# Chunked delta rule on one core: the next chunk's inversion in the same bursts as the current chunk's solution, side work of VectorE cut into single pieces, group norm by three column groups

## The chip, the cores and the metric

The kernel runs as one program on one core of a Trainium2 chip. The metric is the device time of a run in microseconds (us); lower is better. Engines are called PE (TensorE), DVE (VectorE), ACT (ScalarE), POOL (GpSimd) and SP (SyncE, which here issues nearly all transfers).

## The reference, cut to what matters

One decoder layer over 536 tokens: 16 meta tokens and 512 prompt tokens (528, one sequence with a running state) and 8 sample tokens with a state each.

```
proj = rmsnorm(x) @ w_in                 # RWKV columns | retention columns | gates gA, gB
# branch A, RWKV-7, 8 heads of 64, over the tokens t in order:
sa = S @ (-kk_t);  S = S * w_t + sa (x) (kk_t * a_t) + v_t (x) k_t;  y_t = S @ r_t
yn = (y - mean(y)) * rsqrt(var(y) + LNX_EPS)      # per head, the group norm
ya = (yn * lnx_w + lnx_b + bonus) * g
# branch B: retention, multiplied by swish of its gate
merged = sigmoid(gA) * (ya @ w_branch_a) + sigmoid(gB) * (o @ w_branch_b)
x = x + merged @ w_out
x = x + hierarchical_moe(rmsnorm(x))              # top-1 group, top-2 of 16 experts
```

Everything is float32 but for some tables of the routing.

## The kernel before, in words

Activations lie with channels on partitions and tokens in columns; a width of 536 tokens is worked in two halves of 268 columns (`HT`). One SBUF tensor, `arena`, holds nearly everything, so the trace names it everywhere and the rows are told apart by line and shape.

**One list sets the order.** `order()` writes a list of steps; every engine walks the same list and does its part of each step (PE from L796, ACT from L1140, DVE from L1333). Engines keep together by semaphores only. So a step's place in the list is its place in the in-order queue of PE, of ACT and of DVE. DVE waits for the end of nearly each of its own instructions.

**Jobs and banks.** Steps named `j_...` are jobs: matrix products into PSUM bank 0 or 1 in turn, read by ACT or DVE. PE may open job n when job n-2 has been read (`open_job`).

**Fill.** 32 projection half-tiles (`j_proj` for the gates, 8 contraction steps each) and 16 of `j_bb` (branch B, 4 steps each) need nothing from branch A. They are cut into parts (`pre` and the job itself, L792) of two contraction steps, a float32 matmul of 268 columns each, which the trace records as two; so a part is four records. There are 160 parts. `take(n)` puts the next n of them into the list. They cover the waits of branch A.

**Branch A** runs over 9 chunks (`CHUNKS`: eight of 64 tokens, one of 16). For each chunk c:

- `wk_prep` (issued one chunk ahead): ACT makes two exponentials of the decays, DVE makes four scaled products from them; `wk_k` holds two more (`decayed`).
- `wk_a` (PE L925 to L943, DVE L1485): products of the scaled keys, and two transposes; DVE masks them into `tp` and `ab`.
- `wk_x` and `wk_t` (L961; L971 and L974) for b = 2, 4, 8, 16: the inverse of a unit triangular 32x32 matrix by doubling. PE's 32x32 products of `wk_x` go through DVE (mask, `xl`) to `wk_t`, whose result DVE adds into `tp`, for the next `wk_x`. `wk_k` puts four transposes behind the first `wk_t`.
- `wk_r`, `wk_sa`, `wk_y`, `wk_sb` (L986 to L1016): right-hand side and solution, block by block, each going through ACT (`rr`, `sa`) or DVE (`y1`) before the next.
- `wk_s` (L1026 to L1044): new state `st` (DVE) and output y (ACT).

A new chunk's `wk_a` waited for everything of the chunk before it, since `tp`, `ab`, `kq` and `tok` exist once. In the list one part of fill stands between each two of these steps (three behind `wk_a`). What the small products of one such place take on PE is called a burst here; an unshared 64-token chunk has 13 of them.

**Side work.** The eight sample tokens' state update (`sm_in`, `j_sk`, `j_sv`, `sm_y`, `j_sy` for four pairs of heads, on DVE 128x512 each) is put into the chunks by `take` at ends of jobs, `sm_in` as three DVE instructions in one step. From chunk 6 on it is followed by the group norm of the first 268 columns: `j_mean` and `j_var` (L1062, sums over a head by a matmul), where DVE subtracts and squares, ACT takes the root, DVE takes the reciprocal and does three more passes (L1576 to L1583), all in one step for each of four pairs of heads and each half.

**Behind the chunks**: the rest of the side work, the group norm of the second half, then `j_ba` (branch A's projection, L1075, 8 tiles for each half of the columns, each read and merged by two DVE instructions), then `j_out`, routing and the experts. `w_ba` is loaded when the last chunk is done; the x of the residual and `w_out` behind it.

## Time and profile before

| | |
|---|---|
| median of 3 runs | 997.94 us (996.11, 997.94, 1003.03) |
| time of the profiled execution | 1003.03 us |
| its span, first to last instruction | 1001.1 us |
| its mean granted PE clock | 0.940 |
| busy: PE, DVE, ACT, POOL | 901.9 us (90%), 390.6 (39%), 211.9 (21%), 37.6 (4%) |
| PE L792, projections and fill, 268 columns, float32 | 1600 records, 417.4 us busy, 410 ns each |
| DVE TENSOR_TENSOR out of PSUM, nine forms | 235, 101.8 us busy, 434 ns each, 291.7 us idle before them |
| DMA | 118.81 MB, mean 119 GB/s |

The span in 40 slices of 25 us: busy tenths of PE and DVE, and the granted clock of PE in tenths of full speed.

```profile
PE   5999999898999999899889999978899954999995
DVE  3422055256448843432443443233651134211125
PEclk9999998699899999999999999957899985999998
```

"Busy" of an engine counts its instructions, not its waits. A granted clock of 0.5 over a stretch means that PE ran at 1.2 GHz there, 1.0 that it ran at 2.4 GHz; values between are mixtures. Branch A's chunks begin at 362.8 us (slice 15) and `j_ba`'s second half starts at about 732.2 us.

### The profile page before, as it was taken

Reading aid. Unit: us, or ns where it says so; the run is one execution under the profiler, and the core shown is the slowest. Engines: PE = TensorE matmul, PEld = TensorE weight load, DVE = VectorE, ACT = ScalarE, POOL = GpSimd, SP = SyncE. Lnnn points to the kernel's source line nnn. Section 1 sums busy time; section 2 is a strip of 40 time slices with the busy share of each in tenths; the row PEclk is TensorE's granted clock in tenths of the full one; section 3 lists DMA queues with packets and bytes.
Section 4 is the critical chain, followed back from the end, with each engine's and each line's share of the span. In section 5 each row is a group of like instructions: output and inputs, shape, how many; then the busy total and the mean of one; then the engine's idle time right before and its main releaser. Section 6 shows DMA issues by size and latency. Waiting matters only on the chain. (4 is left out here: it accounts for less than half of the span.)

```text
span 1001.1 us, 20286 instructions
## 1 busy us (share of the span) xinstructions
PE 901.9 (90%) x8942; PEld 620.3 (62%) x8942; DVE 390.6 (39%) x742; ACT 211.9 (21%) x423; POOL 37.6 (4%) x34
## 2 busy tenths in 40 slices
PE   5999999898999999899889999978899954999995
PEld 4777756676667867676667767746688841333331
DVE  3422055256448843432443443233651134211125
ACT  2000210114332122221222132222200240111124
POOL 0000000000000000000000000000000001122223
PEclk9999998699899999999999999957899985999998
DMA  9111101201111111001110100106406228999976
GB/s 357 68 64 61 66 21 43 116 1 64 66 60 59 55 36 34 27 30 34 34 33 34 45 24 24 44 22 218 176 3 270 84 84 316 417 386 392 396 260 223
DMA packets 26998, 118.81 MB, mean 119 GB/s; under 512 B 5328, under 2 KB 7632, under 8 KB 22048
## 3 DMA queue, kind: packets, MB, share of 16 engines
q1 hardware_dynamic: 22592, 106.57, 27.9%
q0 software_dynamic: 4320, 10.95, 3.8%
q8 instruction: 71, 1.16, 0.5%
q14 instruction: 15, 0.12, 0.0%
HBM read 104.24 MB, written 18.05 MB: 122 GB/s over the span
## 5 line engine op out<-in xcount | busy, mean ns | idle before, releaser
L792 PE MATMUL psum<-arena 128*128 128x268 f32 x1600 | 417.4, 410 | 9.4 <-ACT arena L1136 5.8
L792 PEld LDWEIGHTS psum<-arena 128*128 128x128 f32 x1600 | 301.6, 196 | 84.8 <-ACT arena L1136 12.6
L1315 DVE TENSOR_TENSOR arena<-psum,arena 128x268 f32<-128x268 f32 (+8 forms) x235 | 101.8, 434 | 291.7 <-PE psum L1075 58.2
L1136 ACT ACTIVATE arena<-psum 128x268 f32<-128x268 f32 (+6 forms) x174 | 72.1, 419 | 527.9 <-PE psum L792 274.3
L1315 DVE TENSOR_TENSOR arena<-arena 128x268 f32<-128x268 f32 (+10 forms) x212 | 105.7, 498 | 68.8 <-ACT arena L1136 56.2
L1075 PE MATMUL psum<-arena 128*128 128x268 f32 x384 | 92.4, 397 | 2.9 <-DVE arena L1315 2.7
L1828 PE MATMUL psum<-arena 128*32 128x512 f32 (+1 forms) x640 | 87.4, 609 | 5.1 <-DVE arena L1981 5.1
L1075 PEld LDWEIGHTS psum<-arena 128*128 128x128 f32 x384 | 72.9, 193 | 19.4 <-DVE arena L1315 4.5
L1981 DVE TENSOR_TENSOR arena<-psum,arena 128x256 f32<-128x256 f32 (+1 forms) x36 | 24.0, 691 | 110.6 <-ACT arena L1895 106.1
L1828 PEld LDWEIGHTS psum<-arena 128*32 128x32 f32 (+1 forms) x640 | 25.6, 117 | 63.4 <-issue 59.4
L1136 ACT ACT_TABLE_LOAD x36 | 46.2, 1283 | 31.4 <-PE psum L792 21.0
L1318 DVE SCALAR_TENSOR_TENSOR arena<-arena 128x268 f32<-128x268 f32 (+4 forms) x93 | 46.4, 499 | 2.7
L1742 POOL DMA_INDIRECT arena<-u_rows,ids x12 | 12.4, 1036 | 895.4 <-DVE ids L2017 833.5
L1860 PE MATMUL psum<-arena 128*32 128x512 f32 (+1 forms) x288 | 40.2, 595 | 0.0
L1318 DVE SCALAR_TENSOR_TENSOR arena<-psum,arena 128x268 f32<-128x268 f32 x24 | 10.5, 439 | 63.5 <-PE psum L819 47.2
L1234 ACT ACTIVATE arena<-psum 64x256 f32<-64x256 f32 (+1 forms) x54 | 20.4, 378 | 64.3 <-PE psum L950 32.7
L961 PEld LDWEIGHTS psum<-arena 32*32 32x32 f32 (+1 forms) x1072 | 11.8, 105 | 22.4 <-issue 13.5
L971 PE MATMUL psum<-arena 32*32 32x32 f32 (+1 forms) x800 | 12.0, 195 | 15.1 <-DVE arena L1315 15.0
L971 PEld LDWEIGHTS psum<-arena 32*32 32x32 f32 (+1 forms) x800 | 9.1, 109 | 26.5 <-DVE arena L1315 20.4
L1860 PEld LDWEIGHTS psum<-arena 128*32 128x32 f32 (+1 forms) x288 | 10.8, 115 | 21.3 <-issue 21.3
L1580 DVE RECIPROCAL arena<-arena 128x268 f32<-128x268 f32 x8 | 14.6, 1829 | 23.6 <-ACT arena L1136 23.4
L1136 ACT ACTIVATE arena<-psum,arena 128x268 f32<-128x268 f32 (+2 forms) x37 | 19.0, 535 | 20.8 <-PE psum L804 10.5
(181 smaller groups left out, 727.0 us busy)
## 6 DMA issues: line engine op xcount, KB each, us to landing
arena<-in_w_gu SPq DMA_DIRECT2D x16, 2048.0 KB, 21.6
arena<-in_w_in SPq DMA_DIRECT2D x46, 512.0 KB, 3.5
arena<-in_w_dn SPq DMA_DIRECT2D x16, 1024.0 KB, 19.3
...
```

The costliest lines, as they stand in the source:

```text
L792: last = mm(ps, wt[:, i % NW, k, :], rhs[:, k, cols(hf)], start=(k == 0), stop=(k == nk - 1))
L971: mm(psum[g, 2560 + H * p:2560 + H * p + n], tp[g, 1, p, 0:n], xl[g, p, 0:n], start=True, stop=True)
L1075: last = mm(ps, w[:, m, k, :], x[:, k, cols(hf)], start=(k == 0), stop=(k == nk - 1))
L1136: run(nc.scalar.activation(out, in_, fn, **kw), s)
L1234: nc.scalar.activation(tok[part, i, :, :], src, ACT.Copy).then_inc(s_toks if s else s_act, 1)
L1315: run(v.tensor_tensor(out, a, b, op), s)
L1318: run(v.scalar_tensor_tensor(out, a, sc_, b, op0, op1), s)
L1580: run(v.reciprocal(x, x))
L1742: pool.indirect_dma_start(ug[:, e % 2, :], None, u2_dram, bass.IndirectOffsetOnAxis(ap=ids[:, e:e + 1], axis=0), bounds_check=T - 1, oob_i ...
L1828: last = mm(bank(2 + i % 2)[part], ue[:, i % 2, k, part], w_gu[x % NWE][:, k, :], start=(k == 0), stop=(k == KD - 1))
L1860: last = mm(bank(down_bank(e) + q)[part], hht(e)[:, f, part], w_dn[x % NWE][:, f, 512 * q:512 * q + 512], start=(f == 0), stop=(f == 1))
L1981: v.tensor_tensor(out, x, y, op).then_inc(s, 1)
```

## The change

It does six things.

1. **Two chunks at once.** `tp`, `ab`, `kq`, `tok` get a second buffer, and the output of `wk_y` moves to another PSUM bank. The solution and the state of chunk c (`wk_r`, `wk_sa`, `wk_y`, `wk_sb`, `wk_s`) are no longer behind its own inversion but inside that of chunk c+1: `wk_x` 2 with `wk_r`, `wk_t` 2 and `wk_k` with `wk_sa`, `wk_x` 4 with `wk_y`, `wk_t` 4 with `wk_sb`, `wk_x` 8 with `wk_s`. A 64-token chunk has 9 bursts then. The last chunk's solution stands alone behind it.
2. **Fill.** 16 parts for each chunk where there were 15: two at five of the nine places, three behind `wk_a`, one behind `wk_x` 4, `wk_t` 8 and `wk_x` 16; 6 instead of 8 before the first `wk_a`.
3. **`wk_prep` and `wk_k` on DVE in single instructions**: `wk_p` 0 to 3 and `wk_d` 0 and 1, one or two per place; the two exponentials (`wk_e`) stand behind `wk_sa`. The decayed old state (`wk_sp`) has a step of its own.
4. **Side work in single instructions**: `sm_in` becomes `sm_a` 0 to 2, the second instruction of each sample job becomes `sm_b`, `sm_c`, `sm_d`. At most one goes to a place (up to three behind the last `wk_t`).
5. **Group norm by three column groups** (`UNITS`): columns 0 to 268 for each pair of heads, 268 to 512 for two pairs at once, and the last 24 columns of all four: 7 `j_mean` and 7 `j_var` instead of 8 and 8. The square moves from DVE to ACT. The reciprocal is cut into pieces (`ln_r`, 134 or 122 columns), and the passes behind it (`ln_w`, `ln_b`, `ln_g`) are single steps. `j_ba` of the second half waits for all seven units.
6. **`w_ba` in two transfers**: the first half, 1 MB, when `j_bb` is done, the second where the whole was.

```
-        w_ba = at(KD * NP * P, KD, NP, P, start=raw0)
+        tp = [at(2 * NP * H, 2, NP, H), tp2]
+        ab = [at(NP * 2 * C, NP, 2, C), ab2]
+        kq = [at(NP * 2 * C, NP, 2, C), kq2]
+        tok = [at(3 * NP * C, 3, NP, C), tok2]
+        w_ba = [at(2048, KD // 2, NP, P, start=x) for x in (base - 4 * T - RH * T, raw0)]
...
+UNITS = [(p, p + 1, 0, HT) for p in range(NP)] + [(0, 2, HT, SEQ), (2, 4, HT, SEQ), (0, NP, SEQ, T)]
+PIECES = [2] * NP + [4, 4, 1]
...
-        s += [("wk_a", c)] + take(3)
-        if c + 1 < len(CHUNKS):
-            s += [("wk_prep", c + 1)]
-        for b in LEVELS[1:]:
-            if b < w:
-                s += [("wk_x", c, b)]
-                if 2 * b >= min(w, H):
-                    s += [("wk_r", c)]
-                s += take(1) + [("wk_t", c, b)]
-                if b == 2:
-                    s += [("wk_k", c)]
-                s += take(1)
-        s += [("wk_sa", c)] + take(1)
-        if w > H:
-            s += [("wk_y", c)] + take(1) + [("wk_sb", c)] + take(1)
-        s += [("wk_s", c)] + take(1)
+        s += [("wk_a", c + 1)] + take(3, 1)
+        s += [("wk_x", c + 1, 2)] + r + take(2, 1)
+        s += [("wk_t", c + 1, 2), ("wk_k", c + 1)] + sa + ([("wk_sp", c)] if c >= 0 else [])
+        s += ([("wk_e", c + 2)] if c + 2 < len(CHUNKS) else []) + take(2, 1)
+        s += [("wk_x", c + 1, 4)] + y + take(1)
+        s += [("wk_t", c + 1, 4)] + sb + prep(c + 2, ("wk_p", 0)) + take(2, 1)
+        s += [("wk_x", c + 1, 8)] + st + prep(c + 2, ("wk_p", 1)) + take(2, 1)
+        if c == 5:
+            while not whole_job():
+                s += take(1)
+            s += [("j_var", n) for n in range(NP)]
+            side += [x for n in range(NP) for x in norms(n)]
+        s += [("wk_t", c + 1, 8)] + prep(c + 2, ("wk_d", 0)) + take(1)
+        if 16 in lev:
+            s += [("wk_x", c + 1, 16)] + prep(c + 2, ("wk_p", 2)) + take(1)
+            s += [("wk_t", c + 1, 16)] + prep(c + 2, ("wk_p", 3), ("wk_d", 1)) + take(2, 1) + beside(3)
...
+    side += [("j_mean", 4), ("j_mean", 5)]
+    s += r + take(2, 2) + sa + [("wk_sp", len(CHUNKS) - 1)] + take(2, 2) + st
+    side += [("j_mean", 6), ("j_var", 4), ("j_var", 5)] + norms(4) + [("j_var", 6)] + norms(5) + norms(6)
...
                 elif kind == "wk_r":
                     pe.wait_ge(s_st, c + 1)
-                    pe.wait_ge(s_toks, 3 * c + 3)
+                    pe.wait_ge(s_toks, 3 * c + (5 if c + 1 < NCH else 3))
...
                 elif kind == "wk_y":
                     pe.wait_ge(s_sa, 2 * c + 1)
+                    pe.wait_ge(s_tri, 3 * c + 6)
...
                 elif kind == "wk_s":
                     pe.wait_ge(s_sa, 2 * c + (2 if CHUNKS[c][1] > H else 1))
+                    if c + 1 < NCH:
+                        pe.wait_ge(s_toks, 3 * c + 6)
...
                     if kind == "j_ba":
-                        pe.wait_ge(s_ba, 16)
-                        pe.wait_ge(s_ya, NP * (hf + 1))
+                        pe.wait_ge(s_ba[m // 4], 16)
+                        pe.wait_ge(s_ya, len(UNITS) if hf else NP)
```

The order of PE's matmuls from the last transposes of a chunk on, before. L792 is fill; a row's x2 is a part (a matmul here is two records of the trace). L961 is `wk_x`, L971 and L974 `wk_t`, L950 `wk_k`, L1051 a sample job. First the beginning of chunk 2's inversion:

```order
L943 MATMUL psum<-arena 64x128 x8
L792 MATMUL psum<-arena 128x268 x6
L961 MATMUL psum<-arena 32x32 x16
L792 MATMUL psum<-arena 128x268 x2
L971 MATMUL psum<-arena 32x32 x16
L974 MATMUL psum<-arena 32x32 x16
L950 MATMUL psum<-arena 64x128 x4
L792 MATMUL psum<-arena 128x268 x2
L961 MATMUL psum<-arena 32x32 x16
```

and the end of the same chunk, where L1000 is `wk_sa`, L1008 `wk_y`, L1016 `wk_sb`, each with fill on both sides:

```order
L974 MATMUL psum<-arena 32x32 x16
L792 MATMUL psum<-arena 128x268 x2
L1000 MATMUL psum<-arena 32x64 x8
L792 MATMUL psum<-arena 128x268 x2
L1008 MATMUL psum<-arena 32x64 x8
L792 MATMUL psum<-arena 128x268 x2
L1016 MATMUL psum<-arena 32x64 x8
L792 MATMUL psum<-arena 128x268 x2
```

The same engine after the change, in chunk 2's inversion from `wk_t` 2 on, with chunk 1's solution in it (L852 is fill, L1023 `wk_x`, L1033 and L1036 `wk_t`, L1012 `wk_k`, L1064 `wk_sa`, L1073 `wk_y`, L1081 `wk_sb`):

```order
L852 MATMUL psum<-arena 128x268 x4
L1033 MATMUL psum<-arena 32x32 x16
L1036 MATMUL psum<-arena 32x32 x16
L1012 MATMUL psum<-arena 64x128 x4
L1064 MATMUL psum<-arena 32x64 x8
L852 MATMUL psum<-arena 128x268 x4
L1023 MATMUL psum<-arena 32x32 x16
L1073 MATMUL psum<-arena 32x64 x8
L852 MATMUL psum<-arena 128x268 x2
L1033 MATMUL psum<-arena 32x32 x16
L1036 MATMUL psum<-arena 32x32 x16
L1081 MATMUL psum<-arena 32x64 x8
```

`wk_sa`, `wk_y` and `wk_sb` have moved into bursts of the next chunk, and there are two parts of fill where there was one, but for the place between `wk_x` 4 and `wk_t` 4.

DVE at such places. Before, between the masks of `wk_a` in chunk 4 and the mask of its first `wk_x` (the 128x128 row), with the semaphores waited for; first the two instructions of a sample job, then four rows of `wk_prep` for chunk 5, waiting for ACT by `s_e`:

```order
L1315 TENSOR_TENSOR arena<-psum,arena 128x512 [waits s_job]
L1568 TENSOR_REDUCE arena<-arena 128x8 [waits s_free0]
L1315 TENSOR_TENSOR arena<-arena 128x256 [waits s_ps,s_e,s_ys]
L1315 TENSOR_TENSOR arena<-arena 128x256 [waits s_dve]
L1318 SCALAR_TENSOR_TENSOR arena<-arena 128x4x64 [waits s_dve]
L1315 TENSOR_TENSOR arena<-arena 128x4x64 [waits s_dve]
L1315 TENSOR_TENSOR arena<-psum,arena 128x128 [waits s_pt,s_ab]
```

After, from the mask of `wk_x` 4 in chunk 3 to that of `wk_x` 8 (the two 128x128 rows):

```order
L1385 TENSOR_TENSOR arena<-psum,arena 128x128 [waits s_pt]
L1385 TENSOR_TENSOR arena<-psum,arena 128x256 [waits s_py,s_rr,s_xl]
L1385 TENSOR_TENSOR arena<-psum,arena 128x256 [waits s_pr]
L1385 TENSOR_TENSOR arena<-arena 128x256 [waits s_e,s_tt]
L1385 TENSOR_TENSOR arena<-arena 128x512 [waits s_free1,s_dve]
L1385 TENSOR_TENSOR arena<-psum,arena 128x128 [waits s_pt,s_ws]
```

The one instruction that waits for the exponentials now stands behind the add of `wk_t` 4, with one piece of side work after it; `wk_prep` is no longer ahead of a mask as a block.

PE behind the chunks, before (L1062 is `j_mean` and `j_var`, L1075 `j_ba` and `j_out`):

```order
L792 MATMUL psum<-arena 128x268 x8
L1075 MATMUL psum<-arena 128x268 x4
L1062 MATMUL psum<-arena 128x268
L1075 MATMUL psum<-arena 128x268 x4
L1062 MATMUL psum<-arena 128x268
```

and after (L1126 `j_mean`, L1131 `j_var`, L1143 `j_ba` and `j_out`), from the last chunk's `wk_s` on:

```order
L852 MATMUL psum<-arena 128x268 x6
L1126 MATMUL psum<-arena 128x96
L1131 MATMUL psum<-arena 128x488 x2
L852 MATMUL psum<-arena 128x268 x8
L1143 MATMUL psum<-arena 128x268 x4
L1131 MATMUL psum<-arena 128x96
L1143 MATMUL psum<-arena 128x268 x76
```

Only 14 matmuls of fill (seven parts) are left behind `wk_s` of the last chunk, where 44 were.

## Rows read from the trace of the kernel before

**Rows 1.** Table by stretch: start:end, length, busy us (count) per engine, PE clock, DMA share.

```profile
362.80:650.00 287.20, 267.23 (x5644) 200.17 (x5644) 111.69 (x249) 71.84 (x147) 0.00 (x0) 0.98 0.10 33
650.00:655.20 5.20, 1.45 (x10) 0.90 (x8) 3.56 (x5) 1.97 (x4) 0.00 (x0) 1.00 0.00 0
655.20:683.00 27.80, 25.08 (x238) 17.24 (x239) 5.09 (x10) 5.73 (x8) 0.00 (x0) 0.51 0.10 31
683.00:711.80 28.80, 24.56 (x97) 18.47 (x96) 11.90 (x18) 8.46 (x12) 0.00 (x0) 0.94 0.49 179
711.80:732.20 20.40, 17.55 (x63) 13.14 (x62) 16.50 (x27) 3.14 (x5) 0.00 (x0) 0.83 0.60 216
850.00:1001.10 151.10, 135.66 (x1030) 47.09 (x1022) 37.76 (x57) 34.58 (x65) 34.21 (x27) 0.97 0.90 346
```

**Rows 2.** Waits of PE, 362.8 to 732.2 us: total us, times, longest.

```profile
PE psum L971 <- DVE arena L1315: 15.0, 10, 3.1
PE psum L961 <- DVE arena L1315: 6.6, 3, 3.8
...
PE psum L792 <- ACT arena L1136: 1.8, 4, 1.0
```

**Rows 3.** PE in order of time, chunk 2: start, duration, instruction, idle before.

```profile
443.52 0.45 PE L961 MATMUL psum<-arena 32*32 32x32 f32 x32
443.90 1.17 PE L792 MATMUL psum<-arena 128*128 128x268 f32 x4
447.50 0.65 PE L971 MATMUL psum<-arena 32*32 32x32 f32 x32 [2.43 <-DVE arena L1315]
```

**Rows 4.** DVE over the same stretch.

```profile
445.31 0.89 DVE L1315 TENSOR_TENSOR arena<-arena 128x256 f32<-128x256 f32 x2 [2.98 <-ACT arena L1136]
...
447.16 1.02 DVE L1315 TENSOR_TENSOR arena<-psum,arena 128x128 f32<-128x128 f32 x2
```

**Rows 5.** ACT over the same stretch.

```profile
443.20 1.28 ACT L1136 ACT_TABLE_LOAD   x1
444.49 0.73 ACT L1136 ACTIVATE arena<-arena 128x256 f32<-128x256 f32 x2
```

**Rows 6.** DVE groups, 362.8 to 732.2 us: busy us, mean ns, idle before.

```profile
L1315 DVE TENSOR_TENSOR arena<-arena 128x512 f32<-128x512 f32 x24 | 16.6, 692 | 2.1 <-ACT arena L1136 1.4
...
L1315 DVE TENSOR_TENSOR arena<-psum,arena 128x128 f32<-128x128 f32 x45 | 13.2, 293 | 31.0 <-PE psum L974 15.5 <-PE psum L961 14.7
```

**Rows 7.** PE in order of time, bursts and fill without waits.

```profile
426.04 1.17 PE L792 MATMUL psum<-arena 128*128 128x268 f32 x4
427.14 0.45 PE L974 MATMUL psum<-arena 32*32 32x32 f32 x32
...
440.71 2.88 PE L792 MATMUL psum<-arena 128*128 128x268 f32 x12
...
453.26 0.45 PE L971 MATMUL psum<-arena 32*32 32x32 f32 x32
453.54 0.48 PE L974 MATMUL psum<-arena 32*32 32x32 f32 x32
...
460.10 0.45 PE L961 MATMUL psum<-arena 32*32 32x32 f32 x32 [1.36 <-DVE arena L1315]
460.49 0.33 PE L986 MATMUL psum<-arena 64*64 64x64 f32 x4
```

**Rows 8.** DVE groups of the group norm, 650 to 732 us, columns as above.

```profile
L1580 DVE RECIPROCAL arena<-arena 128x268 f32<-128x268 f32 x8 | 14.6, 1829 | 23.6 <-ACT arena L1136 23.4
L1318 DVE SCALAR_TENSOR_TENSOR arena<-arena 128x268 f32<-128x268 f32 x16 | 8.0, 499 | 0.6
```

**Rows 9.** ACT in order of time: two roots of the group norm.

```profile
684.98 0.86 ACT L1136 ACTIVATE arena<-psum,arena 128x268 f32<-128x268 f32 x2
```

**Rows 10.** PE in order of time, behind the chunks: one `j_ba`.

```profile
711.79 1.97 PE L1075 MATMUL psum<-arena 128*128 128x268 f32 x8
713.60 0.61 PE L1062 MATMUL psum<-arena 128*128 128x268 f32 x2
```

337 lines of the change are left out of this document (202 added, 135 removed).

## Prediction

> **What bounds the kernel now.** The page first: PE is busy for 901.9 of 1001.1 us, DVE for 39%, ACT for 21%. So the time is PE's own work, plus its waits, plus what it loses where its clock is granted at half. The change touches one stretch, from the first chunk at 362.8 us to the second half of `j_ba` at 732.2 us, and the table by stretch [rows 1] cuts it in five. Length less busy time gives PE's idle time: 20.0, 3.7, 2.7, 4.2 and 2.9 us, 33.5 together. The clock column gives the rest. A clock of 0.98 over 287.2 us loses 2% of it, 5.7 us. Between 655.2 and 683 us it is 0.51, nearly all at 1.2 GHz, though PE is busy for 25.1 of 27.8 us: 0.49 x 27.8 = 13.6, less half of the 2.7 us in which PE did nothing anyway, 12.3 us. The fall stands behind the longest wait (3.8 us, [rows 2]). The last two stretches lose 0.06 x 28.8 = 1.7 and 0.17 x 20.4 = 3.5, less half of some idle time, 2.8. Low clock: 22.5 us. Waits and clock make 56.0 us, the most that better cover can give back.
>
> Whom PE waits for says the list of waits [rows 2]: DVE, at `wk_t` (L971, ten times, 15.0 us) and `wk_x` (L961, 6.6 us). One such wait in order of time shows why. PE ends a part of fill and is ready for `wk_t` at 445.07, but starts at 447.50 [rows 3]. DVE's mask for it is the first of two instructions at 447.16 [rows 4]. Ahead of that mask stands `wk_prep`, four instructions that begin at 445.31 after 2.98 us of waiting for ACT. ACT was loading its table and making the two exponentials, 443.20 to 445.22 [rows 5]. So a 0.29 us mask is late because a block of four instructions and a chain through ACT stand in front of it in an in-order queue; elsewhere it is the block of `sm_in`. DVE is not short of time, its work is in the wrong order.
>
> **The change, part by part.**
>
> *The waits in the chunks (20.0 us idle, 5.7 us clock).* The exponentials now follow `wk_sa` and their first reader stands behind the add of `wk_t` 4. Between the two PE does two parts of fill, `wk_x` 4 with `wk_y`, one part, and `wk_t` 4: 2.0 + 0.7 + 1.1 + 0.6 = 4.4 us with fill at 1.0 to 1.1 and a small product at 0.3 to 0.4 [rows 7], against ACT's 1.2 us for three copies (0.37 each if they cost as an exponential) and 2.0 us for load and exponentials [rows 5]. Covered. DVE's longest queue between a product and the next that needs it: behind `wk_x` 2 mask 0.29, mask of `kq` 0.69 and one piece 0.69, 1.7 us [rows 6], while PE does `wk_r` and two parts (2.0). Behind `wk_x` 4, `wk_t` 8 and `wk_x` 16 only one part, 1.10 us from start to start (426.04 to 427.14, [rows 7]), covers a mask of 0.29 or an add of 0.44 [rows 4] and the product of `wk_prep` behind it, 0.9 us at most. That holds, but with 0.2 us to spare. The three pieces behind the last `wk_t` (2.1 us) have two parts and 3.5 us of `wk_a` above them. The shared bursts add waits for ACT: `wk_r` for the four copies of the new chunk, made during three parts of fill, and `wk_y` for the copy behind `wk_sa`, two parts earlier. Both are done. I leave 4 us of the 25.7: the 1.8 us for ACT at banks [rows 2], which sample jobs between two fills still cause, and 2.2 us for places with 0.2 us to spare. Bounds: 1.8, and half of the 20.0, 10.
>
> *Fewer bursts.* A part alone takes 1.10 us, but three in a row 2.81 (440.71 to 443.52), 0.94 each: going over from small tiles to 128x128 costs 0.16. Thirty-two records of 32x32 products take 0.38 before fill (443.52 to 443.90), but 0.28 with more such products behind them (453.26 to 453.54): 0.10 for going the other way [rows 3, 7]. So 0.26 us for a burst with its stretch of fill, 0.13 for a border. With 13 bursts becoming 9 that would be 4 x 0.26 x 8 chunks = 8.3 us. But a burst that mixes tile sizes keeps borders inside: `wk_x` is followed by `wk_r` after 0.39 us (460.10 to 460.49), as long as by fill [rows 7]. Counting changes of tile size, a chunk had 22 and has 16: 6 x 0.13 x 8 = 6.2 us. I take 6.2. The Trainium skill (TensorEngine Tiling, Key Properties) says that "changing tiling mode (not just tile) drains the TensorE", which speaks against a part of this change, since three of the five shared bursts change mode inside. By the rule the gain is 6.2 us, without it 8.3; the 0.39 us row agrees with the rule.
>
> *The stretch of low clock (3.7 and 2.7 us idle, 12.3 us clock).* The wait of 3.8 us at 651.5 us came from `j_var` of the first half: reciprocal 1.83, two passes 1.03, product 0.44, one block of 3.3 us [rows 4, 8], in front of a mask. After, that is five instructions of 0.9 us or less, one for a place at most times. The wait goes, and I take it that the clock then stays up: all 18.7 us. In its place come four `j_var` in a row in chunk 6. Banks 0 and 1 alternate, so the third waits until ACT has read the first, behind the reading of the projection (0.4), a table load (1.28) and a root (0.43 to 0.5, [rows 5, 9]): 2.2 us after the projection's end, with 1.1 us of PE work before (two jobs): 1.2 us lost.
>
> *Behind the chunks (7.1 us idle, 4.5 us clock).* Laid out from T, the end of the last but one half-tile of fill. PE does `j_mean` 6 (0.2), waits 0.3 for ACT to have read the fill, does `j_var` 4 and 5 (0.95 each, two banks of nearly 500 columns) and is ready at T + 2.4. The bank comes free with ACT's root: reading 0.4, square 0.2, table load 1.28, root of 488 columns about 0.65 [rows 5, 9], with gaps T + 2.8. So 0.7 us lost. Four parts more (3.7) end at T + 6.5, and the eight `j_ba` of the first half, 1.81 us each (711.79 to 713.60, [rows 10]), with `j_var` 6 at T + 21.2. DVE begins at T + 2.8: reciprocals of 976 columns at 1829/268 = 6.8 ns, 6.7 us [rows 8]; of 96 columns, 0.7; eight passes over 244 columns at 0.44, 3.5; two products of 488, 1.3; nine short instructions for the 24 columns, 1.4; sixteen of 0.44 for `j_ba`, 7.0; and 45 gaps of 0.03, 1.4. That is 22.0 us, to T + 24.8. PE waits 0.7 us at the second `j_ba`, since the block of unit 4 stands ahead of the first one's reader, and then 24.8 - 21.9 = 2.9 us for the last unit, before `j_ba` of the second half. Waits: 0.7 + 0.7 + 2.9 = 4.3 us. PE was slow behind a wait of 2.4 us (L971 took 0.65 where 0.45 is usual, [rows 3, 7]), so 2.0 us of clock more. Bounds of the two together: 2 and 10. `j_mean` and `j_var` take 0.6 us less in all, two starts of a job.
>
> By the Trainium skill (ScalarE: Activation LUTs, What ACT_TABLE_LOAD costs) a load comes with a drain, 2.66 us in all. The row shows 1.29 us from load to the next instruction [rows 5]; by the page's figure the two roots above would come 1.4 us later each, an estimate of 2.8 us more. I go by the row.
>
> *Transfers and the beginning.* The 1 MB of `w_ba` goes ahead of a projection tile that is wanted two tiles of fill later. Its second half has some 15 us. With six parts instead of eight `wk_a` starts as DVE's products end; nothing lost or won. Experts are loaded after `j_ba` and `j_out`, so their transfers move up with the rest.
>
> **Sum.** Given back 33.5 + 22.5 + 6.2 + 0.6 = 62.8 us. New or left: 4 + 1.2 + 4.3 + 2.0 = 11.5 us. Net 51.3 us. The profiled execution took 1003.03 us, the slowest of the three (median 997.94); since most of what differs between runs should lie in waits and clock that now go, I count from 1003.03 itself: 951.7 us, or 952.
>
> **The rivals.**
>
> *Forecast, chance 0.70.* With its own bounds: chunk waits 1.8 to 10, tail 2 to 10, clock of the first stretch +-1.4, borders 6.2 to 8.3: 942 to 964.
>
> *The waits move (0.19).* Single cover of 1.10 us fails where a piece of side work or of the norm stands in front of the mask, or the tail is DVE-bound: seven parts of fill are left behind the chunks where 22 were, and DVE's 22 us stand against 18.8 us of PE work. For it: the 0.2 us margin. Against it: DVE has 12 us of work in a chunk of 31. If half of the chunk waits stay (10 and 3 of clock instead of 4) and the tail waits as long as before (7.1 + 4.5 instead of 6.3), that is 9 + 5.3, about 966; with the low clock of 27.8 us coming back at one wait over 3 us, up to 978.
>
> *The clock stays low whatever the order (0.05).* PE was busy nine tenths of the 27.8 us and did not get its clock back [rows 1]. If low stretches belong to the small products and not to the wait, the 22.5 us stay: 952 + 22 = 974.
>
> *No gain (0.03).* The last stage moves its data at 0.90 DMA share [rows 1]. If those transfers did not move up with the rest, the gain would vanish there: about 1000. Against: nothing in it is issued by time, all behind semaphores of `j_ba` or `j_out`.
>
> *Slower (0.03).* Five shared bursts per chunk tie the chain through ACT to the inversion. If each waited for ACT, the 51 us would be gone at 51/40 = 1.3 us each, the length of one table load [rows 5] ahead of a copy; at 1.8 us each, 952 + 72 = 1024 us.
>
> **How the numbers follow.** The likeliest case gives 952. Reaching up into the second case until about 2 in 10 are left out, and down to the forecast's own lower bound, the range is 941 to 968. About 1% is what a measurement of this kernel can tell from no change: faster by over 1% means under 988, which the first three cases give: 0.94; within 1% 0.03; slower 0.03.
>
> **What would show it.** The chunks' PE waits for DVE fall from 20 to under 6 us in 280; no stretch of 20 us stands at 0.5; a chunk has nine bursts and takes about 31 us; the longest PE wait is at the first `j_ba` of the second half, for `ln_g`, about 3 us. Wrong would be: waits of over 1 us at `wk_x` or `wk_t` in most chunks, PE waiting for ACT at `wk_r` or `wk_y`, or low clock without a wait in front.

## The result, and the profile after

| kernel | median us | lowest to highest | profiled run | its span | its mean clock |
|---|---|---|---|---|---|
| before | 1000.49 | 996.11 to 1006.0 | 1003.03 | 1001.1 | 0.940 |
| after | 961.94 | 957.59 to 969.43 | 963.45 | 961.9 | 0.954 |

The ratio is 0.962, with a 95% interval from 0.954 to 0.970. The change takes 38.6 us off the median and 39.6 us off the profiled run. The forecast was 952 us, 51.3 us less than the profiled run of before. So the sign and the range (941 to 968) held, and 11.7 us of the forecast gain, over a fifth, stayed out. Where they went can be read from the trace.

The table by stretch of after, from the first chunk to the end of `j_ba`, columns as in [rows 1]:

```profile
361.60:500.00 138.40, 138.10 (x2894) 106.20 (x2895) 70.04 (x145) 40.53 (x79) 0.00 (x0) 1.00 0.12 37
500.00:512.00 12.00, 9.50 (x146) 6.37 (x145) 2.61 (x6) 4.37 (x7) 0.00 (x0) 0.72 0.01 1
512.00:560.00 48.00, 47.91 (x1071) 37.87 (x1070) 18.53 (x43) 11.00 (x24) 0.00 (x0) 1.00 0.19 63
560.00:595.00 35.00, 30.98 (x596) 23.02 (x594) 9.28 (x23) 12.76 (x23) 0.00 (x0) 0.95 0.11 33
595.00:650.00 55.00, 55.00 (x1140) 43.18 (x1140) 25.13 (x55) 14.14 (x33) 0.00 (x0) 1.00 0.10 31
650.00:667.00 17.00, 16.51 (x129) 11.21 (x127) 2.02 (x4) 4.58 (x9) 0.00 (x0) 0.80 0.40 120
667.00:692.20 25.20, 18.80 (x82) 15.37 (x83) 22.48 (x44) 4.17 (x6) 0.00 (x0) 0.99 0.71 268
692.20:772.80 80.60, 80.60 (x371) 65.53 (x372) 15.76 (x44) 6.89 (x10) 0.00 (x0) 0.96 0.27 111
```

The first 138 us of the chunks run without a gap and at full clock: PE is busy for 138.10 of 138.40 us, where the whole chunk stretch of before had 20.0 us of idle time at a clock of 0.98 [rows 1]. The stretch of 27.8 us at 0.51 is gone. What is left sits in three places, which the list of waits of after names (361.6 to 692.3 us; total, times, longest, as in [rows 2]):

```profile
PE psum L1143 <- DVE arena L1385: 6.1, 2, 4.9
PE psum L852 <- ACT arena L1204: 3.3, 3, 2.5
PE psum L1126 <- ACT arena L1204: 2.9, 1, 2.9
PE psum L1131 <- ACT arena L1204: 1.4, 2, 1.1
```

L1143 is `j_ba`, L852 fill, L1126 and L1131 `j_mean` and `j_var`. No `wk_x` or `wk_t` is in the list. PE waits for ACT in the chunks instead. PE in order of time around 504 us, and ACT over the same stretch:

```profile
499.56 1.17 PE L852 MATMUL psum<-arena 128*128 128x268 f32 x4
500.57 1.02 PE L1118 MATMUL psum<-arena 128*128 128x512 f32 x2
504.09 2.15 PE L852 MATMUL psum<-arena 128*128 128x268 f32 x4 [2.50 <-ACT arena L1204]
```

```profile
499.90 0.39 ACT L1204 ACTIVATE arena<-psum 128x256 f32<-128x256 f32 x1
500.31 1.28 ACT L1204 ACT_TABLE_LOAD   x1
501.60 0.73 ACT L1204 ACTIVATE arena<-arena 128x256 f32<-128x256 f32 x2
502.35 1.28 ACT L1204 ACT_TABLE_LOAD   x1
503.64 0.40 ACT L1204 ACTIVATE arena<-psum 128x268 f32<-128x268 f32 x1
```

The fill at 499.56 ends a half-tile of projection, and ACT is to read it with a sigmoid so that the bank comes free. A sample job follows at once, then the next half-tile, which wants that bank. ACT has just begun `wk_e`: table load, two exponentials, table load back. The reader starts at 503.64, and PE goes on at 504.09 after 2.50 us of waiting, with the clock down (the next part of fill, four records, takes 2.15 us instead of 1.17). The same picture stands in chunk 6 at 571.10 us, where `j_mean` waits 2.91 us.

The third place is the end of the first half of `j_ba`, PE in order of time:

```profile
664.91 1.91 PE L1131 MATMUL psum<-arena 128*128 128x488 f32 x4 [0.29 <-ACT arena L1204]
667.35 3.88 PE L852 MATMUL psum<-arena 128*128 128x268 f32 x16 [0.53 <-ACT arena L1204]
...
674.37 12.91 PE L1143 MATMUL psum<-arena 128*128 128x268 f32 x56 [1.14 <-DVE arena L1385]
692.20 13.00 PE L1143 MATMUL psum<-arena 128*128 128x268 f32 x43 [4.92 <-DVE arena L1385]
```

DVE is busy for 22.48 of the 25.2 us before it (the last row but one of the table by stretch).

**A ruler for the experiments.** The medians of one kernel differ by up to 6 us from chip to chip (955.9 and 961.9 for the changed kernel), and the first chunk of these kernels starts anywhere between 363.6 and 372.0 us, though nothing ahead of it differs: between 10 and 300 us the clock varies by itself (0.88 over 100 to 200 us in e0_after; 0.96, 0.87 and 0.96 over 10 to 100, 100 to 200 and 200 to 300 us in e9_norm_late, where e0_after has 1.00 in the first and the last). So beside each median stands the **rest**: the span less the start of the first `wk_a`. Kernels without a long wait repeat it within 0.6 us (e1: 581.2 and 581.3; e5, e6 and e10: 575.7 to 576.3). The changed kernel, whose waits bring low clock in one run and not in another, does not (594.7 and 589.6).

| kernel | median us | ratio, 95% interval | first `wk_a` | rest |
|---|---|---|---|---|
| before | 1000.49 | | 370.31 | 630.8 (two parts of fill, some 2 us, more lie ahead of it) |
| after | 961.94 | 0.962 [0.954, 0.970] | 367.19 | 594.7 |
| e0_after | 955.88 | 0.957 [0.951, 0.962] | 363.62 | 589.6 |
| e1_exp_late | 949.18 | 0.949 [0.944, 0.954] | 365.50 | 581.2 |
| e1_again | 952.08 | 0.950 [0.946, 0.954] | 369.17 | 581.3 |
| e2_apart | 959.49 | 0.961 [0.955, 0.967] | 363.79 | 592.9 |
| e3_norm_early | 960.04 | 0.958 [0.953, 0.963] | 369.25 | 590.9 |
| e5_tail | 944.51 | 0.941 [0.937, 0.945] | 364.47 | 575.7 |
| e6_split | 946.26 | 0.943 [0.937, 0.948] | 368.42 | 576.3 |
| e7_own | 953.26 | 0.950 [0.947, 0.954] | 367.82 | 583.7 |
| e8_blocks | 951.09 | 0.950 [0.948, 0.951] | 369.56 | 581.7 |
| e9_norm_late | 965.32 | 0.962 [0.959, 0.965] | 372.02 | 595.3 |
| e10_spread | 946.19 | 0.944 [0.943, 0.946] | 371.75 | 575.9 |
| e11_own_blocks | 975.82 | 0.977 [0.973, 0.982] | 367.13 | 608.0 |

### The profile page after: what moved, and what is told of

It is laid out like the page before. It is cut to its first block and busy times, and to the rows that moved or that the text cites. A ratio compares the mean times of both kernels' runs of the same rounds, so it can differ in the third digit from the quotient of the medians.

```text
span 961.9 us, 20304 instructions
## 1 busy us (share of the span) xinstructions
PE 882.5 (92%) x8938; PEld 612.1 (64%) x8938; DVE 390.4 (41%) x748; ACT 212.3 (22%) x427; POOL 37.3 (4%) x34
## 5 line engine op out<-in xcount | busy, mean ns | idle before, releaser
L852 PE MATMUL psum<-arena 128*128 128x268 f32 x1600 | 404.2, 404 | 10.8 <-ACT arena L1204 7.3
L852 PEld LDWEIGHTS psum<-arena 128*128 128x128 f32 x1600 | 299.5, 194 | 91.7 <-ACT arena L1204 14.8
L1385 DVE TENSOR_TENSOR arena<-arena 128x268 f32<-128x268 f32 (+11 forms) x203 | 102.1, 503 | 62.4 <-ACT arena L1204 51.6
L1143 PE MATMUL psum<-arena 128*128 128x268 f32 x384 | 92.7, 399 | 6.1 <-DVE arena L1385 6.1
L1143 PEld LDWEIGHTS psum<-arena 128*128 128x128 f32 x384 | 73.6, 195 | 22.0 <-issue 6.6
L1388 DVE SCALAR_TENSOR_TENSOR arena<-arena 128x268 f32<-128x268 f32 (+6 forms) x101 | 48.2, 477 | 3.0
L1204 ACT ACT_TABLE_LOAD x34 | 43.6, 1283 | 10.1 <-DVE arena L1529 7.7
L1388 DVE SCALAR_TENSOR_TENSOR arena<-psum,arena 128x268 f32<-128x268 f32 (+2 forms) x23 | 10.4, 451 | 68.2 <-PE psum L879 47.2
L1204 ACT ACTIVATE arena<-arena 128x256 f32<-128x256 f32 (+11 forms) x56 | 21.8, 412 | 8.3 <-DMA arena<-in_x 3.3
L1984 ACT ACTIVATE arena<-psum 128x256 f32<-128x256 f32 x12 | 4.6, 387 | 84.8 <-PE psum L1917 84.8
L1204 ACT ACTIVATE arena<-psum,arena 128x268 f32<-128x268 f32 (+4 forms) x36 | 18.6, 542 | 13.4 <-PE psum L864 9.9
L1023 PEld LDWEIGHTS psum<-arena 32*32 32x32 f32 (+1 forms) x1072 | 12.1, 108 | 13.0 <-issue 13.0
L1893 PE MATMUL psum<-arena 128*128 128x128 f32 x96 | 13.5, 286 | 6.1 <-DMA arena<-u_rows,ids 6.1
```

Of the source, the lines that this page charges most:

```text
L852: last = mm(ps, wt[:, i % NW, k, :], rhs[:, k, cols(hf)], start=(k == 0), stop=(k == nk - 1))
L1023: last = mm(psum[g, 2304 + H * p:2304 + H * p + n], ab[c % 2][g, p, 0, rd], tp[c % 2][g, 0, p, 0:n], start=True, stop=True)
L1143: last = mm(ps, w[:, k, :], x[:, k, cols(hf)], start=(k == 0), stop=(k == nk - 1))
L1204: run(nc.scalar.activation(out, in_, fn, **kw), s)
L1385: run(v.tensor_tensor(out, a, b, op), s)
L1388: run(v.scalar_tensor_tensor(out, a, sc_, b, op0, op1), s)
```

## The experiments

### Where the missing gain went

**e0_after** is the changed kernel itself.

> The changed kernel itself, for comparison on this chip. Its trace on record shows 13.8 us of PE idle time between 361.6 and 692.2 us and 11.8 us of low clock up to 772.8 us. Both theories expect the same picture: waits for ACT of 2.5 us in chunk 4 and 2.9 us in chunk 6 behind a table load and two exponentials, and 4.9 us for DVE ahead of the second half of the branch projection. A ratio to the kernel before of about 0.96.

It repeats every wait of after within 0.1 us. Its rest is 5.1 us shorter than that of after, because the clock stayed up behind the wait in chunk 4 (34.6 us from `wk_a` to `wk_a` instead of 37.4) and over parts of the tail.

**e1_exp_late** moves the exponentials behind the parts that follow `wk_sa`:

```
-        s += ([("wk_e", c + 2)] if c + 2 < len(CHUNKS) else []) + take(2, 1)
+        s += take(2, 1) + ([("wk_e", c + 2)] if c + 2 < len(CHUNKS) else [])
```

> One change to the changed kernel: the two exponentials of the next chunk stand behind the two parts of fill that follow wk_sa, not ahead of them. My theory: the two new waits of PE (2.5 us in chunk 4, 2.9 us in chunk 6) come from ACT, which must load a table, make the exponentials and load the table back before it reads the projection whose bank PE needs next. Both waits go, and with them the low clock behind them (3.4 and 1.7 us): 10 us less than the changed kernel, within 8 to 11. Rival: the banks are the cause (a job right behind a projection), the reading is late anyway, and the exponentials, now later, hold up DVE's first product: the waits stay at 2 us or more and new ones of about 1 us appear at wk_x 8 in each chunk, 0 to +8 us.

Measured: 949.18 us, 6.7 under e0_after and so less than the 8 to 11 us expected; the rest is 8.3 us shorter. The longest waits of PE in e1_again, the same kernel, 355 to 770 us:

```profile
PE psum L1143 <- DVE arena L1385: 6.1, 2, 4.9
PE psum L961 <- DVE arena L1385: 2.1, 1, 2.1
PE psum L1131 <- ACT arena L1204: 1.4, 2, 1.1
```

The waits of 2.5 and 2.9 us are gone and nothing came in their place (the 2.1 us at L961 stand before the first chunk, in after too). Of the 8.3 us, 6.9 lie in the chunks (247.2 us from the first `wk_a` to the last, against 254.1 in e0_after): 5.4 us of waiting, and the rest low clock behind it. The other 1.4 us lie behind the chunks, where the two kernels are the same. So one position of one step on ACT cost 6.9 us in e0_after, and 9.8 in after (257.0 us), where the clock also fell behind the wait in chunk 4.

**e3_norm_early** begins the norm of units 4 and 5 earlier: their means right behind the state of chunk 7, their variances ahead of the last `wk_s`.

```
+        if c == 7:
+            while not whole_job():
+                s += take(1)
+            s += [("j_mean", 4), ("j_mean", 5)]
...
-    side += [("j_mean", 6), ("j_var", 4), ("j_var", 5)] + norms(4) + [("j_var", 6)] + norms(5) + norms(6)
+    s += [("j_var", 4), ("j_var", 5)] + take(1, 1) + st
+    side += norms(4) + [("j_mean", 6), ("j_var", 6)] + norms(5) + norms(6)
```

> The changed kernel with the means of the 244-column groups right behind the state of chunk 7 (a projection half-tile earlier) and their variances ahead of the last chunk's state. My theory: the 4.9 us wait before the second half of the branch projection and the 1.1 us at its second job come from DVE being the bound there, 22 us of its work starting at the first root; started 5 to 6 us earlier, the two waits fall from 6.0 to about 1 to 2 us and the low clock behind them (3.2 us) goes: 6 us less than the changed kernel, within 3 to 8. Rival: DVE's work is bound by PE's jobs that it must read one after the other, the wait only moves ahead: under 2 us of difference.

A miss: the time is 4.2 us and the rest 1.3 us longer than that of e0_after, and PE still waits 4.73 us ahead of the second half (4.91 in e0_after). The rest alone would be a weak witness here, since the clock behind the last `wk_s` stood at 0.66 over 10 us in this run and at 0.83 in e0_after, which is 1.7 us; the wait that stayed is the finding. DVE in order of time shows why it stayed:

```profile
664.25 0.67 DVE L1391 TENSOR_TENSOR arena<-arena 128x488 f32<-128x488 f32 x1
670.00 0.26 DVE L1394 SCALAR_TENSOR_TENSOR arena<-psum,arena 128x96 f32<-128x96 f32 x1 [5.08 <-PE psum L1132]
672.28 0.44 DVE L1391 TENSOR_TENSOR arena<-psum,arena 128x268 f32<-128x268 f32 x1 [2.03 <-PE psum L1149]
```

DVE finished unit 4 at 664.9 us and then stood still for 5.08 and 2.03 us. Unit 5 was ready, but in program order it stood behind the mean of unit 6 and the first `j_ba`, for which DVE had to wait. Starting work early gains nothing while the queue order puts a later arrival ahead of what comes after it.

**e5_tail** (with e1_exp_late's edit) has the same early jobs and puts the norms of both units beside the last parts of fill, ahead of the mean of unit 6:

```
+    late = norms(4) + norms(5)
+    while fill:
+        s += late[:3] + take(1)
+        del late[:3]
+    s += late
+    side[:] = [("j_var", 6)] + norms(6)
+    s += [("j_mean", 6)]
```

The counter that paces side work beside the last fill and `j_ba` (`credit`) starts at -1.5 here instead of 0.

> The kernel of e1_exp_late once more, as partner for the next two on the same chip: 949 us, ratio 0.949, the wait of 6 us for the units' evictions in the column-group norm's tail still there.

> e1_exp_late, and in the tail the mean jobs of units 4 and 5 go right after the state of chunk 7, their variance jobs ahead of the last wk_s, and the norms of both units all lie beside the last parts of the projections, ahead of the mean of unit 6; only unit 6 is normed beside the first half of j_ba. Theory (VectorE's 24.7 us of work without a gap from the root of unit 4 to the first j_ba of the second half is what PE waits for there, and e3_norm_early left it because unit 5 still stood beside j_ba, with VectorE idle for 7 us before): VectorE ends its work ahead of the second half some 7 us earlier against PE, the wait of 4.9 us and the clock lost behind it (3.4 us in 670 to 690) go, 941 to 943 us. Rival (the wait only moves again, as in e3): PE waits about as long at j_ba's second or third job, whose bank VectorE has not emptied because units 4 and 5 stand ahead of it: 946 to 950 us.

Measured 944.51 us, between the theory's 941 to 943 and the rival's 946 to 950. Its partner e1_again came out at 952.08 on the same chip, 3 us above the 949 that was expected of it; the difference is 7.6 us, as the theory had it, and the rest is 5.6 us shorter. The longest waits of PE in e5_tail, 355 to 770 us, without the one of 9.2 us that belongs to the stage behind:

```profile
PE psum L864 <- ACT arena L1216: 1.1, 2, 0.8
PE psum L1143 <- ACT arena L1216: 1.1, 1, 1.1
PE psum L1155 <- DVE arena L1400: 1.0, 1, 1.0
```

and PE in order of time:

```profile
660.01 2.07 PE L1155 MATMUL psum<-arena 128*128 128x268 f32 x8 [0.98 <-DVE arena L1400]
662.67 32.79 PE L1155 MATMUL psum<-arena 128*128 128x268 f32 x144 [0.39 <-DVE arena L1397]
```

The rest of `j_ba` and the beginning of `j_out`, 144 records, now run in one piece. The theory holds; the rival's wait at the first jobs exists but is 1.0 us. With e1_exp_late's edit and this one the kernel is at 0.941 [0.937, 0.945] of before: the fastest of all, 59 us under the median of before on the same chip (1003.47).

**e10_spread**: e5_tail with the four `j_var` of chunk 6 in two pairs.

> e5_tail with the four variance jobs of chunk 6 in two pairs, one whole projection apart, so that the third need not wait for the root of the first. Theory: the wait of 1.1 us for ScalarE in chunk 6 goes and nothing else moves, about 1 us less than e5_tail, which the time can hardly show; it serves as e5_tail's repetition beside the two above: 942 to 946 us. Rival: the later roots delay the norms into the tail, 1 to 3 us more.

The wait of 1.1 us is gone and the chunk is 36.5 instead of 37.1 us long, but 0.4 us more of waiting stands elsewhere, and the rest is the same (575.9 and 575.7). It can stand as a repetition of e5_tail.

### Which part of the change brings the gain in the chunks

Two things were changed there together: DVE's work in single pieces, and two chunks that share bursts. The next three undo one or both.

**e2_apart** keeps two chunks in flight but gives each solution step a place of its own between two parts of fill, with the same 16 parts. Five steps leave the 9 shared bursts, so it has 14 (the expectation says 13):

```
-        s += [("wk_x", c + 1, 2)] + r + take(2, 1)
+        s += [("wk_x", c + 1, 2)] + take(1, 1) + r + take(1)
```

and so on for the other four.

> The changed kernel with the solution's five steps taken out of the shared bursts: wk_r, wk_sa, wk_y, wk_sb and wk_s each stand alone between two parts of fill inside the next chunk's inversion, 13 bursts for a chunk again with the same 16 parts. Everything else is as in the changed kernel. My theory (a price of 0.13 us for each change of tile size, 6 more in a chunk): a chunk without waits, 30.9 us from wk_a of chunk 2 to that of chunk 3, takes 31.7 us; in all 6 us more than the changed kernel. Rival 1 (the price is for a burst, 0.26 us each): 31.9 us, 8 us in all. Rival 2 (the shared bursts matter because the two parts of fill behind each cover DVE): with single parts DVE waits return, 1 us or more per chunk, 15 us or more in all. Rival 3: sharing brings nothing, 30.9 us.

Chunk 2 is 32.8 us long against 30.9 in e0_after, but it has six products of 128x512 for the sample jobs where that has four. Where both have six (chunk 3: 32.8 and 31.8), and in chunk 5 and 7 (30.2 and 29.2), the difference is 1.0 us for five bursts, 0.20 us each. Rival 1's 31.9 us came true, but for another count: at its price of 0.26 us five bursts would cost 1.3. The theory's 0.13 us for a change of tile size comes closer; five separate bursts have seven changes more, 0.9 us. DVE waits did not return (rival 2). The whole kernel is only 3.6 us slower than e0_after, since the edit also takes away the two waits for ACT; against e1_exp_late, which has none of them either, the stretch from the first `wk_a` to the last is 7.1 us longer (254.3 and 247.2).

Where the 0.20 us come from can be read at one burst, `wk_x` 2 and `wk_r` of chunk 2. Shared, in e5_tail (L1035 `wk_x`, L1062 `wk_r`, L864 fill, L1045 the next `wk_t`), PE in order of time:

```profile
428.82 0.45 PE L1035 MATMUL psum<-arena 32*32 32x32 f32 x32
429.20 0.33 PE L1062 MATMUL psum<-arena 64*64 64x64 f32 x4
...
430.28 2.08 PE L864 MATMUL psum<-arena 128*128 128x268 f32 x8
432.28 0.45 PE L1045 MATMUL psum<-arena 32*32 32x32 f32 x32
```

and apart, in e2_apart (L1023 `wk_x`, L1050 `wk_r`, L852 fill, L1033 `wk_t`):

```profile
428.29 0.45 PE L1023 MATMUL psum<-arena 32*32 32x32 f32 x32
428.67 1.17 PE L852 MATMUL psum<-arena 128*128 128x268 f32 x4
429.77 0.33 PE L1050 MATMUL psum<-arena 64*64 64x64 f32 x4
...
430.85 1.17 PE L852 MATMUL psum<-arena 128*128 128x268 f32 x4
431.95 0.45 PE L1033 MATMUL psum<-arena 32*32 32x32 f32 x32
```

Shared, the whole takes 3.46 us, apart 3.66. All of the 0.20 us is on the side of the fill: two parts in a row take 2.00 us from start to start, two single ones 1.10 each. On the other side nothing is saved, for `wk_x` is followed after 0.38 us, by `wk_r` as by fill. It is otherwise where both steps use 32x32 tiles: the second product of `wk_t` 4 is followed after 0.29 us by `wk_sb` (438.32 to 438.61 in e5_tail) and after 0.41 by fill (438.38 to 438.79 in e2_apart).

**e7_own** solves each chunk in its own turn, as before, with all single pieces kept (and the exponentials late):

```
+    for c in range(len(CHUNKS)):
...
+            s += [("wk_x", c, 16)] + r + prep(c + 1, ("wk_p", 2)) + take(1)
+            s += [("wk_t", c, 16)] + prep(c + 1, ("wk_p", 3), ("wk_d", 1)) + take(1, 1)
+        s += sa + [("wk_sp", c)] + take(1)
+        if w > H:
+            s += y + take(1) + sb + take(1, 1)
```

> The changed kernel with the exponentials late, but each chunk solved in its own turn as in the kernel before, in bursts of its own (14 instead of 9 in a chunk of 64), one part of other work between each; VectorE's side work and the preparation stay in single pieces, the group norm stays by column groups. What is left out of the change is thus only that inversion and solution share bursts. Theory (most of the chunks' gain is VectorE's work in single pieces; sharing only saves borders and leaves more cover): no waits for VectorE over 0.5 us in the chunks, a chunk of 32.5 to 33 us as in e2_apart, against 30.9; 957 to 963 us, thus 8 to 14 above e1. Rival (without sharing the chain through a chunk is too tight for the cover of one part a step): PE waits for VectorE again, 10 us or more over the chunks, 970 to 980 us.

(It has 13 bursts, not 14.) Measured 953.26 us, under the expected 957 to 963, and not the rival's 970 to 980. It is 1.2 us above e1_again, where 8 to 14 were expected. But the edit did more than take the sharing away: 12 parts of fill lie behind the last `wk_s` (48 records) where after has 7 (28), and PE waits for DVE at `j_ba` only 0.7 us in all, where e1_again waits 6.1. Between 366 and 650 us PE waits for DVE nowhere:

```profile
PE psum L856 <- ACT arena L1205: 1.6, 3, 0.6
PE psum L1132 <- ACT arena L1205: 1.1, 1, 1.1
PE psum L1127 <- ACT arena L1205: 0.9, 1, 0.9
```

So the fair partner is e5_tail, whose tail waits about as little; against it the rest is 8.0 us longer. In chunks 5 and 7, where neither kernel has a wait or a sample job, a chunk takes 30.02 us against 29.19, 0.83 us for four bursts, the same 0.21 apiece as in e2_apart and 6.6 us over eight chunks. With DVE's work in single pieces the sharing is worth its bursts and little more.

**e8_blocks** is e5_tail with the preparation in a block of two and one of four, and the three opening instructions of the sample update as one:

```
+        s += prep(c + 2, ("wk_p", 0), ("wk_p", 1))
...
-        s += [("wk_x", c + 1, 8)] + st + prep(c + 2, ("wk_p", 1)) + take(2, 1)
+        s += [("wk_x", c + 1, 8)] + st + prep(c + 2, ("wk_p", 2), ("wk_p", 3), ("wk_d", 0), ("wk_d", 1)) + take(2, 1)
```

> e5_tail with VectorE's side work in blocks again, while inversion and solution go on sharing bursts: the preparation of a chunk in a block of two operations and one of four (they stood one by one), the sample update's three opening operations as one block. With e7_own (single pieces, no sharing) it splits the change in two. Theory (e7_own kept nearly the whole gain, so the single pieces are what took away the chunks' waits): the blocks bring 1 to 2 us of waits for VectorE back in a chunk, 8 to 15 us in all, with low clock behind the longer ones; 953 to 960 us. Rival (either half of the change is enough: with only 9 bursts in a chunk VectorE has two parts of cover at most of them, and a block of four operations of 0.43 us is hidden there): waits under 3 us in all, 944 to 948 us.

Measured 951.09 us; the rest is 6.0 us longer than e5_tail's, between the two. Waits for DVE, 366 to 650 us, at `wk_t` (L1046) and at one sample job in chunk 0 (L1131):

```profile
PE psum L1046 <- DVE arena L1398: 3.3, 3, 1.3
PE psum L1131 <- DVE arena L1398: 1.9, 1, 1.9
```

**e11_own_blocks** is e7_own with the blocks of the kernel before; its group norm and its tail stay those of e7_own.

```
+        s += (prep(c, ("wk_d", 0), ("wk_d", 1)) if c else []) + [("wk_a", c)] + take(3, 1)
+        s += [("wk_e", c + 1)] if c + 1 < len(CHUNKS) else []
+        s += prep(c + 1, ("wk_p", 0), ("wk_p", 1), ("wk_p", 2), ("wk_p", 3))
```

> e7_own with VectorE's work in the blocks of the kernel before: four preparation operations in one block behind the first three parts of a chunk, two at its end, the sample update's three opening operations in one block, and each sample job's eviction with the one or two operations behind it. Both halves of the change in the chunks are undone in it; the group norm by column groups stays, and its tail is that of e7_own. Theory (either half hides most of VectorE's blocks, so only with both undone do the waits return): waits of TensorE for VectorE in the chunks near the 20 us of the kernel before, with low clock behind some, 970 to 980 us, thus 17 to 27 above e7_own, while e8_blocks lost only 6 to e5_tail. Rival (the halves add up independently): 6 us above e7_own, 957 to 962 us.

```profile
PE psum L1041 <- DVE arena L1391: 14.7, 9, 2.8
PE psum L1124 <- DVE arena L1391: 1.9, 1, 1.9
```

(L1041 is `wk_t`, L1124 a sample job.) At `wk_t` the waits of before are back almost to the digit: 14.7 us in nine, where before had 15.0 in ten [rows 2]. The picture in front of them is that of [rows 3] to [rows 5], too: DVE waits for ACT's exponentials, does the preparation as a block, and the mask comes behind. Chunk 3, DVE and PE:

```profile
486.28 0.89 DVE L1391 TENSOR_TENSOR arena<-arena 128x256 f32<-128x256 f32 x2 [3.73 <-ACT arena L1210]
```

```profile
488.48 0.45 PE L1041 MATMUL psum<-arena 32*32 32x32 f32 x32 [2.44 <-DVE arena L1391]
```

The four kernels side by side, by their rest:

| | bursts shared | each chunk by itself |
|---|---|---|
| DVE in single pieces | 575.7 (e5_tail) | 583.7 (e7_own) |
| DVE in blocks | 581.7 (e8_blocks) | 608.0 (e11_own_blocks) |

Undoing one costs 8.0 or 6.0 us, undoing both 32.3. The two are substitutes: either takes away most of the waits, one by making what stands in front of a mask short, the other by giving more fill to hide it. Neither can be credited with the gain alone; single pieces first leave 8.0 us for the sharing, sharing first leaves 6.0 us for the pieces.

The last corner is so high in part because of the clock. Of the 24.3 us between e7_own and e11_own_blocks, 16.6 are waits for DVE, and the clock stands at 0.97 over the 285 us of the chunks, some 8 us, where e7_own has 1.00. Behind four of the nine waits at `wk_t`, those of 2.1 to 2.8 us, the clock fell; behind the five of 1.6 us or less it did not. In e8_blocks, whose waits are 1.0 to 1.9 us long, it did not fall in the chunks at all.

The corners are not quite a clean square. The blocks of e8_blocks are smaller than those of e11_own_blocks: with two chunks in flight the last four instructions of the preparation cannot stand so early, and only e11_own_blocks puts a sample job's second instruction right behind its first; so the 6.0 may be low. In both block kernels the first block also stands right behind the exponentials, while in the kernels with single pieces two more steps of the inversion lie between the exponentials and their first reader; no run separates that distance from the block itself.

**e9_norm_late** is e5_tail with the norm of the first 268 columns where units 4 and 5 stood, and units 4 to 6 beside `j_ba`:

```
-        if c == 5:
-            side += [("j_mean", n) for n in range(NP)]
...
+    late = [x for n in range(4) for x in norms(n)]
+    side[:] = [("j_mean", 6), ("j_var", 4), ("j_var", 5)] + norms(4) + [("j_var", 6)] + norms(5) + norms(6)
```

> e5_tail with the group norm of the first half of the tokens (units 0 to 3) not beside chunks 7 and 8, but where units 4 and 5 stood, and units 4 to 6 behind it beside j_ba. Theory (VectorE's 13.7 us of norm work for those units is hidden by the chunks and nothing but VectorE is the bound from there to the second half of j_ba): the tail gets most of it back as waits of TensorE for VectorE, plus low clock behind them, 12 to 20 us more than e5_tail, 957 to 965 us. Rival (TensorE has enough to do in the tail, the early norm only fills slots): up to 5 us more, 944 to 950 us.

Measured 965.32 us; the rest is 19.6 us longer, at the upper end of the theory's 12 to 20. PE in order of time:

```profile
665.07 5.57 PE L1151 MATMUL psum<-arena 128*128 128x268 f32 x16 [3.60 <-DVE arena L1396]
...
697.35 18.01 PE L1151 MATMUL psum<-arena 128*128 128x268 f32 x66 [12.98 <-DVE arena L1393]
```

So taking the norm of the first half away from the chunks costs more than undoing either half of the change there: DVE is the bound behind the chunks, and 13.7 us of its work put there cost 19.6 us of time, the waits and the low clock behind them. Not all of this is the change's gain: before, two of the four pairs of heads had their norm beside the last chunk already (reciprocals at 651.5 and 667.7 us), and two behind it (685.6 and 689.0).

### The low clock without a wait in front

In after the clock falls at 657 us, within the last `wk_s`, whose products are 16 rows or columns wide, with no PE wait ahead of it. **e6_split** is e5_tail with one part of fill between the two halves of that step:

```
+    s += side + [("j_var", 4), ("j_var", 5)] + take(1) + st + take(1) + [("wk_so", len(CHUNKS) - 1)]
```

> e5_tail, and in the last chunk one part of a projection lies between the matmuls of the state and those of the output, which are 16 rows or columns wide. Theory (the clock fell at 657 us of the changed kernel because of that run of tiny matmuls): with it split the clock stays at full speed there in this run, 0 to 3 us less than e5_tail. Rival (the fall has to do with something else, and comes in some runs only): same time as e5_tail within 1.5 us.

The 10 us from the first product of the last `wk_s` on (length, PE, PEld, DVE, ACT and POOL busy with counts, PE clock, DMA share, GB/s) in e1_exp_late and e3_norm_early, both with the step in one piece:

```profile
643.40:653.40 10.00, 9.18 (x102) 6.94 (x102) 1.47 (x3) 3.92 (x8) 0.00 (x0) 1.00 0.47 143
```

```profile
656.70:666.70 10.00, 10.00 (x97) 8.32 (x97) 6.66 (x10) 1.91 (x3) 0.00 (x0) 0.66 0.47 112
```

The first shows no fall, the second loses a third of its clock with PE busy all the time, and over the same stretch of their own both e6_split and e5_tail stand at 0.83. The step split in two brings nothing (rests 575.7 and 576.3). All in all the fall begins within 6 us of the first product of this step in ten of the thirteen traces of after and its variants; in e1_exp_late, e1_again and e7_own it does not come, and in no trace does the clock fall without a wait anywhere else from the first `wk_a` to the end of `j_out`. So the place is shown and the cause is not: the tiny products stay a suspect, but the same step leaves the clock alone in three traces, two of them of one kernel whose order here is that of after.

## Why the prediction was right, and where it was not

**What bounds the kernel: right.** The idle time of PE and its low clock were the 56.0 us to be had, and DVE's order was the reason. The waits and the low clock of before are gone from all their places in the chunks; chunk 2 takes 30.9 us (424.38 to 455.28), as forecast, without a gap. e11_own_blocks confirms the reading of one wait in the old trace (a mask behind a block of four): with the blocks put back, nine such waits return.

**Clock: right for the long stretch, not for all of it.** The stretch at 0.51 went with the wait ahead of it. "All 18.7 us" was too much: in the same last chunk the clock fell once more, at 657 us, and cost 3.4 us there. That is one of the prediction's own signs of being wrong, low clock without a wait in front. The rival that low clock belongs to the small products (0.05) falls for the 32x32 and 64x64 ones: in e5_tail every window from 360 to 640 us stands at 1.00. For the 16-wide ones of the last `wk_s` it stays open, as above. None of the other signs came: no `wk_x` or `wk_t` waits, PE waits for ACT neither at `wk_r` nor at `wk_y`, and the longest wait stands where it was forecast, ahead of the second half of `j_ba`.

**"Both are done. I leave 4 us": the step that failed.** The list of new waits for ACT looked at the shared steps `wk_r` and `wk_y`, which indeed wait for nothing. It did not look at what else ACT does: in front of the bank that PE wants next stands ACT's read of the last projection, and `wk_e` with both table loads, 1.28 + 0.73 + 1.28 = 3.3 us, was now placed where a job can follow a projection at once. The load's price was right (1.28 us); the load *back*, which the next sigmoid pays, was left out of the sum. It happened in two chunks of nine: 5.4 us of waits and in after 5.2 us of clock (3.4 in 500 to 512, 1.8 in 560 to 595), 10.6 us, where the whole budget for the chunks was 4.

**Four `j_var` in a row: right.** 1.2 us forecast, 1.1 measured.

**The tail: right in kind, low in size.** Forecast were 0.7 us at the root, 0.7 at the second `j_ba` and 2.9 ahead of the second half. The trace has 0.29 + 0.53, 1.14 and 4.92. So PE waited 6.9 us behind the last `wk_s`, hardly less than the 7.1 of before, where 4.3 were forecast. The list of DVE's work held but for the short instructions: eight passes over 24 columns take 2.21 us, 0.28 each with the gap, where nine were put at 1.4 together. And the wait of 4.92 us brought low clock, 3.2 us in 692 to 772 us. The forecast's 2.0 us of clock for everything stands against 12.0 (the clock column of the table by stretch, each row's shortfall times its length).

**Fewer bursts: right.** The prediction chose 0.13 us for each change of tile size, 0.78 a chunk and 6.2 in all, over 0.26 for a burst, 1.04 a chunk. Four bursts more cost 0.83 us a chunk in e7_own, 6.6 in all, and five bursts with seven changes 1.0 us in e2_apart: 0.14 for a change. The parts were a little off (0.20 us instead of 0.16 on the side of the fill). By the rule of the Trainium skill (TensorEngine Tiling, Key Properties) that a change of tiling mode drains the engine, a mixed burst should keep borders inside. These rows agree: `wk_x` goes over to `wk_r` in 0.38 us, as to fill, while `wk_t` goes over to `wk_sb` of its own tile size in 0.29 instead of 0.41.

**The sum.** Losses left or new were 25.8 us (13.8 idle and 8.8 of clock up to 692.2 us, 3.2 of clock behind) where 11.5 were forecast, 14.3 more. PE's own work in the stretch fell by 5.3 us (38.7 less from the first chunk to the second half of `j_ba`, 33.4 of it losses) where 6.8 were forecast, 1.5 short. Against these 15.8 us, 1.2 us came ahead of the first chunk and 2.9 us behind it, where the change does nothing and runs differ anyway. That makes the 11.7 us between 51.3 and 39.6. The 5.3 us hang on how the clock's share is worked out (the forecast took half of the idle time off it, this sum does not); the bursts alone are 6.6 us by e7_own, so the 1.5 us short are not shown to be a fault of their price.

**The rival of waits that move (0.19)** named 966 us and half of the chunk waits. The time fell between it and the forecast. Its first mechanism, cover of 1.10 us that fails in front of a mask, did not occur once; in the chunks the waits moved to another engine. Its second one, a tail bound by DVE that waits as long as before, did occur: 6.9 us against the 7.1 that it named. So the range held with the help of some luck: the loss of 10.6 us in the chunks was of a kind that neither the forecast nor a rival had named.
